# Moving the output gate's projection and the keys' rotation in the first mixer of a two-block transformer

## Chip, cores and metric

One core of a Trainium2 chip runs the whole program. The metric is device time in microseconds, the median of three executions. TensorE is PE in the rows, VectorE DVE, ScalarE ACT, GpSimd POOL, SyncE SP.

## What is computed

The reference is a model of two blocks in float32 on 256 tokens (`x`) with 256 context tokens; later come two more attention layers with experts. The change lies in the first block's mixer alone. There `h` (256 tokens) and `hx` (256 context tokens), both 1024 wide, are multiplied by one matrix of 3600 columns, which gives the queries, keys and values of a neighbourhood attention, those of an mLSTM, an output gate and the mLSTM's input and forget gates:

```python
qa, ka, va, qb, kb, vb, ob, g = jnp.split(h @ w_in, SPLITS, axis=-1)
y_a = neighbourhood_attention(qa, ka, va, kax, vax, rpb)
h_b, _ = mlstm_bidirectional(axial_rope(qb), axial_rope(kb) * k_scale, vb, li, lf, ...)
y = jnp.concatenate([y_a, rms_norm(h_b, head_g) * sigmoid(ob)], -1) @ w_out
```

The mLSTM runs over four chunks of 128 tokens (two of them context) in two directions and with four heads. Per chunk it updates a state by `outer(k * a_tok, v)`, where `a_tok` comes from running sums and maxima of the gates, and then reads it. The output gate `ob` is needed for the 256 tokens of `x` only, and only at the end.

## The kernel before

Everything in float32 goes as two parts (`hh` high, `hl` low; a weight tile as `wh` and `wl`), so each product is three matmuls. The weights stream from memory in the order in which TensorE uses them, in slabs of 16 tiles of 128x128. A slab lands in `raw`, ScalarE copies its high part to `wh` (L1414, `split_upto`) and VectorE subtracts to get `wl` (L2080). There are three buffers of `wh` and `wl`, so slab i is split once slab i-3 has been used. Each engine runs a program written out by hand in one order, and waits on counters of what the others have done. `taken(n)` in the programs of ScalarE and VectorE stands where n tiles begin to be used, and splits the slabs that come three later: where it stands is where those engines do that work.

`mixer0` exists once per engine (TensorE L738, ScalarE L1575, VectorE L2390). On TensorE the order is:

1. query columns `naq` of the attention (`x` only), then its values `nav` (`project_tok`, all 512 tokens), keys `nak` with the attention worked in between, and the gates `mgate`;
2. the mLSTM's queries `mq` (into `mqT`) and keys `mk` (into `mkT`), the rotation of the queries (`rotate("rotq")`: two matmuls with the permutation `swap`, then four VectorE operations), and the values' projection `mv` (to `mva`);
3. `cc`: 20 small transposes of the gates' rows, and `ap`: four small matmuls. They wait for "rows", the end of the running sums and maxima of the gates on VectorE (L2470 to L2480, eight rounds) and of their exponentials on ScalarE;
4. the rotation of the keys (`rotk`), the output gate's projection `og` (two blocks of 128 tokens, 48 matmuls, two slabs), the turning of the rotated keys (`kt`, 16 transposes, L803) and of the attention's results (`turn_out`, 8 transposes, L700);
5. the 16 `outer` products, each of which waits for a scaled key `mKS` of ScalarE (L1650), then the loop over the reads of the state, with the output projection `mout` in between.

Of PSUM there are 8 banks, given out in turn: who takes a bank waits until its last content has been read.

Of the kernel before, what the change touches and what calls it, by code (L numbers as in the profile page):

```python
# [13 lines left out]
P = 128  # L14
D = 1024
KC = 8
# [103 lines left out]
def program(nc, dram):  # L120
# [88 lines left out]
    with ExitStack() as mx:  # L209
# [13 lines left out]
        with ExitStack() as ph:  # L223
# [3 lines left out]
            ml.og = sb(ph, "mog", [P, 2, 512])  # L227
            ml.cs = const(ph, "mlcs", [P, 2, T])
            ml.swap = const(ph, "swap", [P, P])
# [19 lines left out]
            ml.ss = sb(ph, "mss", [P, 3, 8])  # L249
        ml.CR, ml.AR, ml.WR, ml.ER = ml.IR, ml.FR, ml.t1, ml.BR  # L250
# [147 lines left out]
    fold_at = {2: HALF, 3: 0, 4: HALF, 5: HALF, 6: 0}  # L398
# [9 lines left out]
    def tensor_program(e):  # L408
# [303 lines left out]
        def project_tok(name, c0, ncol, blocks, h, by, *key, steps=0):  # L712
# [7 lines left out]

        def h_part(k):
            return hh[:, k, 0:T], hl[:, k, 0:T]

# [14 lines left out]
        def mixer0():  # L738
# [8 lines left out]
            st.kept.remove(bank_of["roots", 1])  # L747
            project_tok("min", 8, 512, 4, h, act_out, "nav")
# [32 lines left out]
            project_tok("min", 20, 512, 4, h, act_out, "mv")  # L781
# [14 lines left out]
            rotate("rotk", ml.kT)  # L796
            project_tok("min", 24, 512, 2, h, act_out, "og")
            result.mark("h read", "mix0")
            for hd in range(4):
                b = bank(("kt", hd), act_out, "kt", hd)  # L800
                w.wait_ge(dve_out, "rotk", "done")
                for ch in range(4):
                    ins = e.transpose(b[:, P * ch:P * ch + P], ml.kT[:, hd, P * ch:P * ch + P], ident[:])  # L803
                ins.then_inc(*result("kt", hd))
# [19 lines left out]
            def weights(i):  # L824
# [5 lines left out]
                sel, k = hh[:, hd, HALF:HALF + P], 4 + 2 * d + ch  # L830
                mm(b[:, 0:2 * P], sel, hh[:, k, 0:2 * P], True, False)
                mm(b[:, 0:2 * P], sel, hl[:, k, 0:2 * P], False, True)
# [20 lines left out]
            def part(d, ks):  # L853
                b = banks[bank_of["mout", d]][:, T * (d % 2):T * (d % 2) + T]
                for k in ks:
                    w.wait_ge(dve_out, "turn l", "mix0", k)
                    wmm(("mout", d, k), b, *h_part(k), k == 0 and d % 2 == 0, k == KC - 1, "mout", d)
# [542 lines left out]
    def scalar_program(e):  # L1400
# [169 lines left out]
        def turn_out(name, c, h_free):  # L1570
            w.wait_ge(result, "turn", name, c)
            w.wait_ge(result, "h read", *h_free)
            e.activation(hh[:, c, 0:T], banks[bank_of["turn", name, c]][:, 0:T], ACT.Copy).then_inc(*act_out("turn h", name, c))

        def mixer0():  # L1575
            taken(4 * KC)
            taken(4 * KC)
# [40 lines left out]
            taken(4 * KC)  # L1618
            w.wait_ge(result, "mv")
# [3 lines left out]
            taken(4 * KC)  # L1623
            w.wait_ge(result, "og")
            for q in range(2):
                act(ml.og[:, q, :], banks[bank_of["og", q]][:], ACT.Sigmoid, key=("og", q))
            for h in range(4):
                w.wait_ge(result, "kt", h)
                act(X[:, h // 2::2, T + P * (h % 2):T + P * (h % 2) + P],
                    banks[bank_of["kt", h]][:].rearrange("p (c k) -> p c k", k=P), ACT.Copy, key=("kt", h))  # L1630

            for c in range(4):
                turn_out("mix0", c, ["mix0"])
            w.wait_ge(const_in["sel4"], 0)
            w.wait_ge(act_out, "rows")
            e.activation(hh[:, 0:4, HALF:HALF + P], ml.sel[:], ACT.Copy).then_inc(*act_out("sel"))
# [1894 lines left out]
```

## Time and profile before

| | us |
|---|---|
| median of three runs | 2453.25 |
| the three runs | 2447.88, 2453.25, 2453.5 |
| profiled execution, its own time | 2445.76 |
| span of its trace | 2444.0 |
| PE busy in it | 2316.0 (95%) |
| DVE busy | 1696.2 (69%) |
| ACT busy | 1197.4 (49%) |
| first mixer, first to last projection | 481 to 740 |

The profiled execution has 1.76 us more than its span. The page gives averages over all stages; since TensorE is busy nearly throughout, what matters for a change in one stage is which gaps TensorE has there, and what ended them. In rows of the trace "[4.72 <-ACT mKS L1650]" says that the engine was idle for 4.72 us and that ScalarE's write of `mKS` ended it; x16 counts instructions that were merged into the row.

### The profile page before, as it was taken

The numbers are of one execution on the slowest core, as the hardware profiler recorded it, in microseconds if no ns is written. First come the engines' busy times: TensorE is split into PE (matmuls) and PEld (weight loads), VectorE is DVE, ScalarE is ACT, GpSimd is POOL, SyncE is SP. The second block draws the span as 40 slices with busy tenths as digits, with TensorE's granted clock in tenths as the row PEclk, the third lists the DMA queues.
The fourth block names the chain that finished last, engine by engine and source line by source line (L and its number), as shares of the span: only waits on it lengthen the run. The fifth ranks groups of instructions, "written<-read, shape, count | busy, mean of one in ns | idle before, by whom it ended". The sixth has DMA issues, their size and how long they took to land.

```text
span 2444.0 us, 33909 instructions
## 1 busy us (share of the span) xinstructions
PE 2316.0 (95%) x14128; PEld 2026.8 (83%) x14128; DVE 1696.2 (69%) x2260; ACT 1197.4 (49%) x1549; POOL 168.0 (7%) x270
## 2 busy tenths in 40 slices
PE   7999999899989999999999998979999889899997
PEld 3778888778779999999999997968888778688886
DVE  5897676743676666666666655568888776688886
ACT  3221212344544454445544454547666666576665
POOL 0111111021000000000000002200000002000000
PEclk9999999999999999999999999989999989999999
DMA  7777887432214454456434454229888732389884
GB/s 277 226 239 254 268 271 257 156 129 99 86 53 156 174 206 170 174 192 227 178 139 173 173 204 141 104 85 354 330 317 322 298 104 71 129 336 348 311 315 167
DMA packets 80534, 501.71 MB, mean 205 GB/s; under 512 B 9584, under 2 KB 10688, under 8 KB 28656
## 3 DMA queue, kind: packets, MB, share of 16 engines
q1 hardware_dynamic: 59120, 423.66, 47.0%
q0 software_dynamic: 21248, 75.75, 9.9%
q8 instruction: 115, 1.88, 0.3%
q14 instruction: 51, 0.42, 0.0%
HBM read 498.33 MB, written 1.05 MB: 204 GB/s over the span
## 4 chain that ended last, share of the span: by engine, by line
PE 65%; DVE 19%; ACT 10%; issue 4%; DMA 1%; DVEq 0%; SPq 0%; ACTq 0%
PE bank L416 63%; DVE wl L2080 8%; ACT wh L1414 6%; DVE macc L2116 1%; ACT s L1515 1%; DVE f L2297 1%; DMA mring<-in_wmod 1%; DVE s L2288 1%; PE bank L653 1%; DMA raw<-in_wmod 1%; DVE rs L2140 1%; PE bank L1286 1%; DVE hl L2272 0%; ACT H L1524 0%; DVE tmpm L2265 0%
## 5 line engine op out<-in xcount | busy, mean ns | idle before, releaser
L2080 DVE TENSOR_TENSOR wl<-raw,wh 128x2048 fp32r<-128x2048 f32 (+1 forms) x437 | 904.9, 2076 | 379.9 <-ACT wh L1414 375.8
L1414 ACT ACTIVATE wh<-raw 128x2048 fp32r<-128x2048 f32 (+1 forms) x437 | 756.4, 1738 | 302.9 <-PE bank L416 302.5
L416 PE MATMUL bank<-hh,wh 128*128 128x258 f32 (+2 forms) x2200 | 688.8, 313 | 32.7 <-ACT o_rl L1843 5.3
L416 PE MATMUL bank<-hh,wl 128*128 128x258 f32 (+2 forms) x2200 | 672.9, 306 | 0.0
L416 PE MATMUL bank<-hl,wh 128*128 128x258 f32 (+2 forms) x2200 | 671.2, 305 | 0.0
L416 PEld LDWEIGHTS bank<-hh,wh 128*128 128x128 f32 x2200 | 419.2, 191 | 63.2 <-issue 7.3
L416 PEld LDWEIGHTS bank<-hl,wh 128*128 128x128 f32 x2200 | 419.7, 191 | 18.2 <-issue 0.5
L416 PEld LDWEIGHTS bank<-hh,wl 128*128 128x128 f32 x2200 | 418.4, 190 | 18.8
L416 PE MATMUL bank<-wh,hh 128*128 128x512 f32 (+1 forms) x704 | 277.6, 394 | 7.6 <-DVE wl L2080 4.7
L416 PE MATMUL bank<-wh,hl 128*128 128x512 f32 (+1 forms) x704 | 274.6, 390 | 0.0
L416 PE MATMUL bank<-wl,hh 128*128 128x512 f32 (+1 forms) x704 | 274.3, 390 | 0.0
L416 PE MATMUL bank<-H,wh 128*128 128x256 f32 (+1 forms) x704 | 219.1, 311 | 2.2 <-DVE L L2307 2.0
L416 PE MATMUL bank<-H,wl 128*128 128x256 f32 (+1 forms) x704 | 217.7, 309 | 0.0
L416 PE MATMUL bank<-L,wh 128*128 128x256 f32 (+1 forms) x704 | 217.7, 309 | 0.0
L2116 DVE SCALAR_TENSOR_TENSOR macc<-mring,c_cvec,macc 128x1024 f32<-128x1024 f32 x140 | 175.7, 1282 | 44.8 <-DMA mring<-in_wmod 39.8
L416 PEld LDWEIGHTS bank<-wh,hh 128*128 128x128 f32 x704 | 133.3, 189 | 40.1 <-issue 5.5
L416 PEld LDWEIGHTS bank<-wl,hh 128*128 128x128 f32 x704 | 133.1, 189 | 29.6
L416 PEld LDWEIGHTS bank<-wh,hl 128*128 128x128 f32 x704 | 133.2, 189 | 27.8 <-issue 0.2
L416 PEld LDWEIGHTS bank<-H,wh 128*128 128x128 f32 x704 | 132.6, 188 | 12.2 <-DVE L L2307 3.1
L416 PEld LDWEIGHTS bank<-H,wl 128*128 128x128 f32 x704 | 132.6, 188 | 8.1
L416 PEld LDWEIGHTS bank<-L,wh 128*128 128x128 f32 x704 | 132.6, 188 | 7.8
L1524 ACT ACTIVATE H<-f 128x256 fp32r<-128x256 f32 (+1 forms) x88 | 41.5, 471 | 192.5 <-DVE f L2304 150.8
(472 smaller groups left out, 2651.1 us busy)
## 6 DMA issues: line engine op xcount, KB each, us to landing
raw<-in_wstream SPq DMA_DIRECT2D x393, 1024.0 KB, 4.9
mring<-in_wmod POOLq DMA_DIRECT2D x128, 512.0 KB, 4.5
raw<-in_wmod SPq DMA_DIRECT2D x6, 1024.0 KB, 6.8
X<-in_xT SPq DMA_DIRECT2D x1, 2048.0 KB, 12.5
mods<-in_wmod SPq DMA_DIRECT2D x2, 1024.0 KB, 19.0
bias<-in_nabias POOLq DMA_DIRECT2D x16, 128.0 KB, 2.5
c_sglg<-in_sglg POOLq DMA_DIRECT2D x1, 1024.0 KB, 4.9
c_sglb<-in_sglb POOLq DMA_DIRECT2D x1, 1024.0 KB, 6.9
```

The source lines that it names most:

```text
L416: return e.matmul(out, lhsT, rhs, start=start, stop=stop, skip_group_check=True)
L653: ins = e.transpose(b[:, P * k:P * k + P], a.E[:, v % 4, P * k:P * k + P], ident[:])
L1286: ins = e.transpose(banks[b][:, P * c:P * c + P], q.H[:, s_, P * c:P * c + P], ident[:])
L1414: e.activation(wh[i % NB][:, o], raw[i % NR][:, o], ACT.Copy).then_inc(*slab_high(st.split + m))
L1515: e.activation(s_, s_, ACT.Silu, bias=f.s[:, i % 2, T:T + 1]).then_inc(*act_out("silu", u, i))
L1524: e.activation(f.H[:, i - f0, :], f.f[:, i % 2, 0:n], ACT.Copy).then_inc(*act_out("H", u, i))
L2080: e.tensor_tensor(wl[i % NB][:, o], raw[i % NR][:, o], wh[i % NB][:, o].bitcast(F32), ALU.subtract).then_inc(*slab_low(st.split + m))
L2116: e.scalar_tensor_tensor(acc, src, c, acc, ALU.mult, ALU.add).then_inc(*dve_out("block", n, who))
L2140: e.reciprocal(rs[:, o:o + T], rs[:, o:o + T]).then_inc(*dve_out("rs", nm, i))
L2288: e.tensor_tensor(f.s[:, i % 2, :], banks[bank_of["fin", u, i, 0]][:, 0:W1], rs[:, 0:W1], ALU.mult).then_inc(*dve_out("rooted a", u, i))
L2297: e.scalar_tensor_tensor(f.f[:, i % 2, 0:T], f.f[:, i % 2, 0:T], f.f[:, i % 2, T:T + 1], f.s[:, i % 2, 0:T], ALU.add, ALU.mult).then_inc(* ...
```

## The change

The projection `og` moves from behind the values' projection to right behind `naq`, and its sigmoid with it on ScalarE. The rotation of the keys moves to TensorE's second step (of eight) of the values' projection, and on VectorE to right behind the rotation of the queries. The turning of the keys moves into the seventh step. On ScalarE the copies of the turned keys come ahead of the values' copies, and the rows' parts ahead of the turned results. Buffers are laid out anew: `og` gets room beside the attention's buffers, the selection rows get a tile of their own (`mrow`), and the turned results use other columns of `hh` and `hl`.

```diff
 # TensorE, mixer0
             st.kept.remove(bank_of["roots", 1])
+            project_tok("min", 24, 512, 2, lambda k: h_of(1, 1, k), act_out, "og")
             project_tok("min", 8, 512, 4, h, act_out, "nav")
...
             rotate("rotq", ml.qT)
-            project_tok("min", 20, 512, 4, h, act_out, "mv")
+            def beside_values(k):
+                if k == 0:
+                    st.kept.update(bank_of["mv", q] for q in range(4))
+                if k == 1:
+                    rotate("rotk", ml.kT)
+                if k == 6:
+                    turn_keys()
+
+            project_tok("min", 20, 512, 4, h, act_out, "mv", middle=beside_values)
...
-            rotate("rotk", ml.kT)
-            project_tok("min", 24, 512, 2, h, act_out, "og")
-            result.mark("h read", "mix0")
-            for hd in range(4):
-                b = bank(("kt", hd), act_out, "kt", hd)
-                w.wait_ge(dve_out, "rotk", "done")
...
 # ScalarE, mixer0
             taken(4 * KC)
+            taken(4 * KC)
+            w.wait_ge(result, "og")
+            for q in range(2):
+                act(ml.og[:, q, :], banks[bank_of["og", q]][:], ACT.Sigmoid, key=("og", q))
...
             act_out.mark("rows")
             taken(4 * KC)
+            w.wait_ge(const_in["sel4"], 0)
+            w.wait_ge(dve_out, "rotk", "done")
+            e.activation(ml.row[:], ml.sel[:], ACT.Copy).then_inc(*act_out("sel"))
+            for h in range(4):
+                w.wait_ge(result, "kt", h)
+                act(X[:, h // 2::2, T + P * (h % 2):T + P * (h % 2) + P],
+                    banks[bank_of["kt", h]][:].rearrange("p (c k) -> p c k", k=P), ACT.Copy, key=("kt", h))
             w.wait_ge(result, "mv")
...
-            taken(4 * KC)
-            w.wait_ge(result, "og")
...
 # VectorE, mixer0
             rotate("rotq", ml.qT)
+            rotate("rotk", ml.kT)
             w.wait_ge(act_out, "softplus", 2)
...
-            rotate("rotk", ml.kT)
-            taken(4 * KC)
```

**VectorE behind the keys' evacuation.** `sq`, `mqT` and `mkT` are the rotations, `mFR` and `mBR` begin the gates' sums. Before:

```order
L2432 TENSOR_SCALAR mkT<-bank 128x512 x4
L2439 TENSOR_TENSOR sq<-bank,c_mlcs 128x512 x2
L2442 TENSOR_TENSOR mqT<-mqT,c_mlcs 128x1024
L2444 TENSOR_TENSOR mqT<-mqT,sq 128x1024
L2449 TENSOR_SCALAR mFR<-mFR 4x1024
L2451 TENSOR_TENSOR mFR<-mFR,mt 4x1024
```

With the change:

```order
L2445 TENSOR_SCALAR mkT<-bank 128x512 x4
L2452 TENSOR_TENSOR sq<-bank,c_mlcs 128x512 x2
L2455 TENSOR_TENSOR mqT<-mqT,c_mlcs 128x1024
L2457 TENSOR_TENSOR mqT<-mqT,sq 128x1024
L2452 TENSOR_TENSOR sq<-bank,c_mlcs 128x512 x2
L2455 TENSOR_TENSOR mkT<-mkT,c_mlcs 128x4x256
L2457 TENSOR_TENSOR mkT<-mkT,sq 128x4x256
L2463 TENSOR_SCALAR mFR<-mFR 4x1024
```

The four operations on `mkT` stood behind the copies to `mCC` and now stand ahead of all work on the gates.

**ScalarE from the last exponential of the gates (`mt`) to the scaled keys (`mKS`).** `wh` are splits of slabs, `X` the turned keys, `mva` the values, `hh<-bank` the turned results. Before:

```order
L1434 ACTIVATE mt<-mMR,mmr 4x128
L1414 ACTIVATE wh<-raw 128x2048 x2
L1621 ACTIVATE mva<-bank 128x4x128 x4
L1414 ACTIVATE wh<-raw 128x2048 x2
L1434 ACT_TABLE_LOAD
L1434 ACTIVATE mog<-bank 128x512 x2
L1434 ACTIVATE X<-bank 128x4x128 x4
L1573 ACTIVATE hh<-bank 128x256 x4
L1636 ACTIVATE hh<-c_sel 128x4x128
L1638 ACTIVATE hh<-mMR 4x4x128
L1638 ACTIVATE hh<-mt 4x4x128
L1650 ACTIVATE mKS<-X,mCC 128x128 x16
```

With the change:

```order
L1446 ACTIVATE mt<-mMR,mmr 4x128
L1426 ACTIVATE wh<-raw 128x2048 x2
L1637 ACTIVATE mrow<-c_sel 128x512
L1446 ACTIVATE X<-bank 128x4x128 x4
L1644 ACTIVATE mva<-bank 128x4x128 x4
L1648 ACTIVATE hh<-mMR 4x4x128
L1648 ACTIVATE hh<-mt 4x4x128
L1585 ACTIVATE hh<-bank 128x256 x4
L1662 ACTIVATE mKS<-X,mCC 128x128 x16
L1670 ACTIVATE mW<-mW 128x128
```

Two splits, a table load and the gate's sigmoids are gone from between, and all the rest is still ahead of the first `mKS`.

**TensorE at the end of the values' projection, with the numbers of the PSUM banks.** With the change (two rows of the seventh step, the turned keys, three of the eighth step, then `cc`, `ap` and the results):

```order
L418 MATMUL bank4<-wh2,hl 128x512
L418 MATMUL bank4<-wl2,hh 128x512
L788 MATMUL bank7<-c_ident,mkT 128x128 x4
L788 MATMUL bank0<-c_ident,mkT 128x128 x4
L788 MATMUL bank5<-c_ident,mkT 128x128 x4
L788 MATMUL bank6<-c_ident,mkT 128x128 x4
L418 MATMUL bank1<-wh2,hh 128x512
...
L418 MATMUL bank4<-wl2,hh 128x512
L809 MATMUL bank7<-c_ident,mIR 128x4
...
L418 MATMUL bank0<-map,c_sel4 128x8 x4
L702 MATMUL bank1<-c_ident,Y 128x128 x2
```

The transposes of `cc` now take bank 7, in which the first head's turned keys lie until ScalarE has copied them to `X`; before they took bank 5, long free, and 48 matmuls of `og` stood behind them. The results `Y` are turned behind `ap`, as before, not inside the values' projection.

## Rows read from the trace of the kernel before

**Rows 1.** The page: span and number of instructions.
```profile
span 2444.0 us, 33909 instructions
```

**Rows 2.** Windows: stretch, us, busy us (count) of PE PEld DVE ACT POOL, clock, DMA.
```profile
496.70:522.00 25.30, 25.30 (x97) 20.32 (x98) 9.90 (x11) 3.03 (x2) 5.53 (x6) 0.88 0.54 187
...
644.60:667.30 22.70, 17.98 (x106) 14.65 (x105) 15.81 (x21) 16.30 (x24) 0.00 (x0) 0.99 0.51 185
```

**Rows 3.** Waits of PE, 480 to 740: us in total, times, longest.
```profile
PE bank L416 <- ACT mKS L1650: 4.7, 1, 4.7
PE bank L416 <- DVE wl L2080: 3.8, 1, 3.8
```

**Rows 4.** Timeline of PE: start, us, engine, line, operation, names, shape, count, idle before.
```profile
620.53 1.96 PE L416 MATMUL bank<-mqT,c_swap 128*128 128x512 f32 x4 [0.83 <-DVE mkT L2432]
...
622.55 0.40 PE L416 MATMUL bank<-wh,hl 128*128 128x512 f32 x1
...
644.62 0.22 PE L789 MATMUL bank<-c_ident,mIR 4*128 4x4 f32 x1
...
646.84 1.98 PE L416 MATMUL bank<-mkT,c_swap 128*128 128x512 f32 x4
...
659.76 1.91 PE L803 MATMUL bank<-c_ident,mkT 128*128 128x128 f32 x16
...
667.26 1.20 PE L416 MATMUL bank<-mva,mKS 128*128 128x129 f32 x4 [4.72 <-ACT mKS L1650]
```

**Rows 5.** Timeline of DVE: the queries' rotation, and the end of the gates' rows.
```profile
621.76 1.45 DVE L2439 TENSOR_TENSOR sq<-bank,c_mlcs 128x512 f32<-128x512 f32 x2 [1.33 <-PE bank L416]
...
624.50 1.22 DVE L2444 TENSOR_TENSOR mqT<-mqT,sq 128x1024 f32<-128x1024 f32 x1
625.83 0.68 DVE L2449 TENSOR_SCALAR mFR<-mFR 4x1024 f32<-4x1024 f32 x1
...
642.07 0.28 DVE L2480 TENSOR_TENSOR mBR<-mBR,mMR 4x128 f32<-4x128 f32 x1
645.41 4.49 DVE L2080 TENSOR_TENSOR wl<-raw,wh 128x2048 fp32r<-128x2048 f32 x2 [3.06 <-ACT wh L1414]
```

**Rows 6.** Timeline of ACT from the end of the gates' rows to the first scaled keys.
```profile
643.48 3.69 ACT L1414 ACTIVATE wh<-raw 128x2048 fp32r<-128x2048 f32 x2
647.20 2.07 ACT L1621 ACTIVATE mva<-bank 128x512 f32<-128x512 f32 x4
649.13 1.94 ACT L1414 ACTIVATE wh<-raw 128x2048 fp32r<-128x2048 f32 x1
...
661.28 1.98 ACT L1434 ACTIVATE X<-bank 128x512 f32<-128x512 f32 x3
...
664.12 1.21 ACT L1573 ACTIVATE hh<-bank 128x256 fp32r<-128x256 f32 x4
665.17 0.66 ACT L1636 ACTIVATE hh<-c_sel 128x512 fp32r<-128x512 f32 x1
665.69 0.61 ACT L1638 ACTIVATE hh<-mMR 4x512 fp32r<-4x512 f32 x1
...
666.73 0.97 ACT L1650 ACTIVATE mKS<-X,mCC 128x128 f32<-128x128 f32 x3
```

**Rows 7.** Timeline of DVE behind the attention's queries: splits of three slabs.
```profile
494.24 4.49 DVE L2080 TENSOR_TENSOR wl<-raw,wh 128x2048 fp32r<-128x2048 f32 x2 [1.32 <-ACT wh L1414]
...
502.50 2.29 DVE L2080 TENSOR_TENSOR wl<-raw,wh 128x2048 fp32r<-128x2048 f32 x1
```

**Rows 8.** Timeline of ACT: table load ahead of the first weights.
```profile
673.83 1.28 ACT L1658 ACT_TABLE_LOAD   x1
675.31 0.31 ACT L1658 ACTIVATE mW<-mW 128x128 f32<-128x128 f32 x1 [0.20 <-DVE mW L2533]
```

**Rows 9.** Windows over the outer products and behind them.
```profile
666.60:673.40 6.80, 6.14 (x27) 6.17 (x28) 5.21 (x14) 5.91 (x16) 0.00 (x0) 0.50 0.00 0
673.40:680.00 6.60, 6.17 (x50) 5.84 (x50) 4.50 (x15) 4.62 (x11) 0.00 (x0) 1.00 0.01 2
```

More of the change, by code:

```diff
@@ L249, in program @@
             ml.ss = sb(ph, "mss", [P, 3, 8])
+            ml.og = sb(ph, "mog", [P, 2, 512])
+            with ExitStack() as pre:
+                ml.cs = const(pre, "mlcs", [P, 2, T])
+                ml.swap = const(pre, "swap", [P, P])
+            ml.row = sb(ph, "mrow", [P, 4, P], F32R)
         ml.CR, ml.AR, ml.WR, ml.ER = ml.IR, ml.FR, ml.t1, ml.BR
@@ L710, in project, with project_tok @@
                         attend(1)
-        def project_tok(name, c0, ncol, blocks, h, by, *key, steps=0):
+        def project_tok(name, c0, ncol, blocks, h, by, *key, steps=0, middle=None):
             bs = [bank((*key, q), by, *key, q) for q in range(blocks)]
@@ L780, in mixer0, with turn_keys @@
             rotate("rotq", ml.qT)
-            project_tok("min", 20, 512, 4, h, act_out, "mv")
+            def turn_keys():
+                for hd in range(4):
+                    b = bank(("kt", hd), act_out, "kt", hd)
+                    w.wait_ge(dve_out, "rotk", "done")
+                    for ch in range(4):
+                        ins = e.transpose(b[:, P * ch:P * ch + P], ml.kT[:, hd, P * ch:P * ch + P], ident[:])
+                    ins.then_inc(*result("kt", hd))
+            def beside_values(k):
[6 more added lines that the diff above has]
+            project_tok("min", 20, 512, 4, h, act_out, "mv", middle=beside_values)
+            st.kept.difference_update(bank_of["mv", q] for q in range(4))
+            result.mark("h read", "mix0")
             b = bank(("cc",), dve_out, "cc")
@@ L1622, in mixer0 @@
                              ACT.Copy).then_inc(*act_out("mv", q))
-            taken(4 * KC)
-            w.wait_ge(result, "og")
[L1625 to L1630, printed above, removed]
-            for c in range(4):
[L1633 to L1636, printed above, removed]
-            for kind, R in enumerate((ml.MR, ml.WR)):
-                e.activation(hh[0:4, 4:8, P * kind:P * kind + P].rearrange("p (d c) t -> p d c t", d=2),
-                             R[:, :, 0:T].rearrange("p d (c t) -> p d c t", c=2), ACT.Copy).then_inc(*act_out("row parts", kind))
+            w.wait_ge(act_out, "rows")
+            for kind, R in enumerate((ml.MR, ml.WR)):
+                e.activation(hh[0:4, 4:8, T + P * kind:T + P * kind + P].rearrange("p (d c) t -> p d c t", d=2),
+                             R[:, :, 0:T].rearrange("p d (c t) -> p d c t", c=2), ACT.Copy).then_inc(*act_out("row parts", kind))
+            for c in range(4):
+                turn_out("mix0", c)
             def scaled_keys(n, unit):
@@ L2495, in mixer0 @@
                           banks[bank_of["ap",]][:, 0:32].rearrange("p (h d s) -> p h d s", d=2, s=4)).then_inc(*dve_out("ap"))
-            rotate("rotk", ml.kT)
-            taken(4 * KC)
+            for kind, R in enumerate((ml.MR, ml.WR)):
+                w.wait_ge(act_out, "row parts", kind)
+                c = slice(T + P * kind, T + P * kind + P)
+                e.tensor_tensor(hl[0:4, 4:8, c].rearrange("p (d c) t -> p d c t", d=2),
+                                R[:, :, 0:T].rearrange("p d (c t) -> p d c t", c=2),
+                                hh[0:4, 4:8, c].rearrange("p (d c) t -> p d c t", d=2).bitcast(F32),
+                                ALU.subtract).then_inc(*dve_out("row parts", kind))
+            for c in range(4):
+                turn_out("mix0", c)
             def update(n, unit):
```

41 lines of the change are left out of this document (15 added, 26 removed).

## Prediction

> **What bounds the kernel now.** The span is 2444.0 us [rows 1], and TensorE is busy for nearly all of it, so I went to the one stage that the change touches and asked where TensorE stands still there. The list of its waits from 480 to 740 us [rows 3] has two that the change can reach. 3.8 us go to a split of a slab (`wl`) right behind the attention's query columns, where `og` now comes in. 4.7 us go to the first scaled key `mKS`, in front of the outer products. The windows [rows 2] show the same: from 644.6 to 667.3 TensorE is busy for 17.98 of 22.70 us, and elsewhere around the moved parts it is full. All else in the stage is TensorE's own work, and the change removes none of it: it is the same matmuls in another order. So the question is only what becomes of the waits.
>
> For the 4.7 us the timelines are read side by side. TensorE rotates the queries at 620.53, runs the 96 matmuls of the values, begins `cc` at 644.62, rotates the keys at 646.84, turns them from 659.76, and starts the outer products at 667.26 [rows 4]. VectorE ends the queries' rotation at 625.72, works on the gates from 625.83, and its last operation there starts at 642.07 [rows 5]. ScalarE ends the gates' exponentials and goes on to the slabs at 643.48, and scales the first key at 666.73 [rows 6]. So the gates' rows are ready 1.1 us before TensorE asks for them at 644.62: that chain, rotation, gates, exponentials, is as long as the values' projection, and `og` behind it gives ScalarE 11 us in which to do everything else.
>
> **The change, part by part.**
>
> *Size of `og`.* From the second matmul of the values at 622.55 to `cc` at 644.62 there are 95 steps, 0.232 us each [rows 4]. 48 such are 11.1 us. As a check: rotation of the keys and `og` take 659.76 - 646.84 = 12.92 us, a rotation takes 622.55 - 620.53 - 0.23 = 1.8 us, and 11.1 are left.
>
> *`og` in its new place: 11.1 us later for all behind it, and no more.* It starts where the values `nav` started, at the same slab, so the wait of 3.8 us stays as it is. The stretch of lower clock behind that wait (0.88 over 496.7 to 522.0 [rows 2]) lasts, I take it, as long with `og` under it. `og` uses a slab in half the time of `nav`: 24 matmuls. The first is used up no sooner than 5.6 us after 496.7 at full clock (24 x 0.232), the second is split at 494.24 + 4.49 = 498.7, the third at 502.50 + 2.29 = 504.8 [rows 7], and it is wanted no sooner than 496.7 + 11.1 = 507.8. So the splits keep ahead by 3 us or more. What if not: one split of 2.29 us is lost. Nothing is gained either, bound 0. The gate's sigmoids, 1.3 us and a table load of 1.28 us on ScalarE, lie beside `nav`.
>
> *VectorE: the gates' rows come 7.4 us later.* The keys' rotation now stands ahead of the gates on VectorE, and it cannot begin until TensorE's `swap` matmuls, which stand behind two of eight steps of the values. The 25th matmul would start at 622.55 + 23 x 0.232 = 627.9. From the start of the `swap` matmuls to the end of the rotation it is 625.72 - 620.53 = 5.2 us [rows 4, 5]. That ends at 633.1, and the gates' first operation starts at 633.2 instead of 625.83: 7.4 us later, of which about 3.3 are VectorE standing still and the rest its work. The gates' chain itself is unchanged, so VectorE's and ScalarE's ends of it move by the same 7.4 us.
>
> *ScalarE: from the end of the gates to the first scaled key.* Before, 666.73 - 643.48 = 23.25 us, mostly waiting for `og` and its sigmoids. Now everything stands in one row behind the gates, in ScalarE's order: two slabs 3.72 (643.48 to 647.20), the selection rows 0.52, the turned keys 4 x 0.66 (1.98 for 3), the values 1.93 (647.20 to 649.13), the rows' parts 1.04 for two, the turned results 1.05 (664.12 to 665.17) [rows 6]. That is 10.9 us.
>
> *TensorE behind the values.* It ends them, with rotation and turning inside (1.8 and 1.9 us), at 644.62 + 3.7 + 11.1 = 659.4. `cc` waits for the gates and also, since it takes the bank of the first turned keys, for ScalarE's copy of them: 643.48 + 7.4 + 11.1 = 662.0 for the slabs, then 3.72 + 0.52 + 0.66, so 666.9. TensorE stands still for about 7.5 us there, then again between the turned results. The results are turned into the banks of the values as ScalarE empties them; the last of these is empty 2.1 us before ScalarE asks for the results, so this hides. `cc` and `ap` take 2.2 us at full clock (644.62 to 646.84); at half clock up to 4.5, which makes the turned results late by 0.5 us at most. Bound: 0 and 0.5; I take 0, as 20 transposes of 4 columns each have little in them that a clock could slow. VectorE's copies of `cc` lie beside ScalarE's values.
>
> *Sum.* The first scaled key, and with it the outer products and all behind, moves by 7.4 (gates) + 10.9 (new row on ScalarE) - 23.25 (old) + 11.1 (`og` ahead of it) = **+6.2 us**. Against the profiled execution's own 2445.76 this is 2452.0. That execution is below all three runs shown, and 7.5 us below their median; on the median 2453.25 it gives **2459.5**, 0.25% more. About 0.3%, or 7.4 us, is what a measurement can tell from no change, so the likeliest finding is "the same", on the slow side.
>
> *The table load.* ScalarE's load at 673.83 goes away, since the sigmoid no longer stands between the exponentials. It ends at 675.11, and the row behind it starts at 675.31 and was released by VectorE's `mW`, not by the load [rows 8]. I take 0; the other bound is 1.28 us. The Trainium skill ("ScalarE: Activation LUTs", "What ACT_TABLE_LOAD costs") gives 2.66 us for each switch of a set, load and drain together; by it the sum would be +3.5. The row speaks against that here: it fits between two instructions that wait for others.
>
> *Clock.* The outer products run at 0.50 of the clock before, 1.2 GHz [rows 9]; TensorE stood still for 4.72 us ahead of them. With 7.5 us of standing still and then a few small matmuls I expect the same again. There 27 matmuls took 6.14 us, two to a product, so 0.45 us a product and 7.3 for 16. If the clock were back for them, this would go down at most to ScalarE's pace of 0.33 (0.97 for 3 [rows 6]), 5.3 us: 2.0 less. If it stayed low longer, the stage behind, 6.60 us at full clock [rows 9], would lose a part: its waits for other engines hide some, so up to 2.
>
> **The rivals.**
>
> - *The clock is back before the outer products.* +6.2 - 2.0 = +4.2 us. For it: `cc`, `ap` and the results keep TensorE active ahead of them. Against: before, it was still at 0.50 up to 673.4, though TensorE had worked densely from 667.26 on [rows 4, 9].
> - *The page's rule on table loads holds.* +3.5 us, from above; against it the row of the load.
> - *More is lost.* A late slab in the early part (2.3) or a low clock for longer (up to 2): about +8.3 us. For it: the longer gap; against: 3 us of room in the splits.
> - *Faster: TensorE is the bound behind the values.* If the gates' rows are done before the values' projection ends, the wait for `mKS` shrinks: ScalarE has only values, rows' parts, results and the key ahead (1.93 + 1.04 + 1.05 + 0.53 = 4.6 us) from TensorE's end at 659.4, so outer products at 664.0 instead of 667.26: -3.3 us. That needs ScalarE done with gates, slabs and turned keys by 659.4. The rows put this at 668.9 (662.0 + 3.72 + 0.52 + 2.64), 9.5 us too late. It decides from the point where VectorE's gates would start 9.5 us sooner, which no row shows.
> - *The change doesn't do what it says:* the results are turned behind `ap`, not inside the values' projection, as the order shows. This is in the sum.
>
> **How the numbers follow.** Forecast 0.60, clock back 0.12, table rule 0.03, more lost 0.18, faster 0.07. The forecast's own spread is 1 us, and a median of three moves by some 2.5 us: the runs of before alone span 5.6 us. From the forecast's +6.2 to the bound of 7.4 it is 1.2 us, so some 0.35 of its chance falls above; of "more lost" some 0.75. That gives slower 0.36. Faster by over 7.4 us comes only from the faster case with a lucky median: 0.02. The rest is 0.62. The range goes from the faster clock with the low runs, 2452, to "more lost" with the high ones, 2465.5; the faster case and the two tails are left out.
>
> **What would show it.** Right: on VectorE the keys' rotation at about 639 to 644 us with idle time ahead of it, and the gates' first operation about 18.5 us later than before (644.3); TensorE's wait at `cc` of 7 to 8 us, released by ScalarE's `X`; the wait for `mKS` smaller than 4.7; the outer products at about 673.4; the early wait of 3.8 us unchanged, no gap inside `og` or `nav`; stages behind 740 us shifted and not changed. Wrong: `cc` following the values without a gap (then the gates' chain is not what bounds), a new wait for `wl` from 497 to 534, or a change of over 2 us behind the mixer.

## The result, and the profile after

| | before | after |
|---|---|---|
| median of 16 runs of each, us | 2450.77 | 2457.03 |
| the runs, us | 2443.49 to 2455.99 | 2450.7 to 2459.47 |
| ratio, 95% interval | | 1.0026 [1.0019, 1.0034] |
| span of the profiled execution, us | 2444.0 | 2454.0 |

The changed kernel is 6.3 us slower by the medians. The two profiled spans are 10.0 us apart, and the trace says how much of that is the change's. The attention's first query column starts at 482.78 us instead of 481.29, and nothing ahead of it was changed. From there to the last product with the gate on VectorE (`Y<-Y,mog`, the end of what the change touches) it takes 240.34 us instead of 235.67. From that product to the end of the span it is 1730.9 instead of 1727.0. So 4.7 us lie in the stage of the change, and 5.3 outside it. How much of either is chance is shown under the experiments.

The page of the changed kernel, its first lines:

```profile
span 2454.0 us, 33910 instructions
...
PE 2322.7 (95%) x14128; PEld 2033.8 (83%) x14128; DVE 1697.2 (69%) x2260; ACT 1195.7 (49%) x1548; POOL 167.9 (7%) x270
```

The waits of PE from 480 to 750 us, the counterpart of [rows 3]. Lines have moved: L418 is the old L416, L2092 the old L2080, L1662 the old L1650, L809 the first small transpose of `cc`.

```profile
PE bank L809 <- ACT X L1446: 7.5, 1, 7.5
...
PE bank L418 <- DVE wl L2092: 3.7, 1, 3.7
...
PE bank L418 <- ACT mKS L1662: 0.8, 1, 0.8
```

The reader is to see that the wait for the first scaled key has almost gone, 4.7 to 0.8 us, and that a larger one has taken its place 6.7 us ahead of the first outer product. The wait of 3.7 for `wl` is nearly as before. It ends where the gate's projection now starts, and behind it the list of PE's waits is empty up to 536 us, so neither this projection nor the one behind it met a late slab.

Timeline of PE, the queries' rotation to the outer products, the counterpart of [rows 4]:

```profile
631.69 1.96 PE L418 MATMUL bank<-mqT,c_swap 128*128 128x512 f32 x4 [0.83 <-DVE mkT L2445]
...
638.98 1.88 PE L418 MATMUL bank<-mkT,c_swap 128*128 128x512 f32 x4
...
654.60 1.91 PE L788 MATMUL bank<-c_ident,mkT 128*128 128x128 f32 x16
...
666.82 0.26 PE L809 MATMUL bank<-c_ident,mIR 4*128 4x4 f32 x1 [7.52 <-ACT X L1446]
...
670.75 1.97 PE L702 MATMUL bank<-c_ident,Y 128*128 128x128 f32 x8
...
673.48 6.95 PE L418 MATMUL bank<-mva,mKS 128*128 128x129 f32 x32 [0.76 <-ACT mKS L1662]
```

VectorE and ScalarE beside it, the counterparts of [rows 5] and [rows 6]. VectorE's timeline, with the keys' rotation now ahead of the gates:

```profile
635.67 1.22 DVE L2457 TENSOR_TENSOR mqT<-mqT,sq 128x1024 f32<-128x1024 f32 x1
640.10 1.48 DVE L2452 TENSOR_TENSOR sq<-bank,c_mlcs 128x512 f32<-128x512 f32 x2 [3.21 <-PE bank L418]
...
642.88 1.22 DVE L2457 TENSOR_TENSOR mkT<-mkT,sq 128x1024 f32<-128x1024 f32 x1
644.21 0.68 DVE L2463 TENSOR_SCALAR mFR<-mFR 4x1024 f32<-4x1024 f32 x1
```

ScalarE's timeline, the row of work from the end of the gates' exponentials to the first scaled keys:

```profile
661.86 3.69 ACT L1426 ACTIVATE wh<-raw 128x2048 fp32r<-128x2048 f32 x2
665.46 0.61 ACT L1637 ACTIVATE mrow<-c_sel 128x512 fp32r<-128x512 f32 x1
666.16 2.66 ACT L1446 ACTIVATE X<-bank 128x512 f32<-128x512 f32 x4
668.72 2.06 ACT L1644 ACTIVATE mva<-bank 128x512 f32<-128x512 f32 x4
670.63 0.61 ACT L1648 ACTIVATE hh<-mMR 4x512 fp32r<-4x512 f32 x1
671.15 0.61 ACT L1648 ACTIVATE hh<-mt 4x512 fp32r<-4x512 f32 x1
671.67 1.47 ACT L1585 ACTIVATE hh<-bank 128x256 fp32r<-128x256 f32 x4
673.04 0.97 ACT L1662 ACTIVATE mKS<-X,mCC 128x128 f32<-128x128 f32 x3
```

No row here shows idle time of ScalarE ahead of it: ScalarE is the chain. TensorE's 7.52 us are the time in which it has nothing to do and ScalarE works off what stands behind the gates.

Windows (stretch, us, busy us and count of PE, PEld, DVE, ACT, POOL, clock, DMA), first over the early part, the counterpart of [rows 2], then over this stretch, the counterpart of [rows 9]:

```profile
496.90:522.00 25.10, 23.91 (x97) 19.42 (x98) 14.46 (x13) 8.61 (x7) 6.77 (x8) 0.93 0.66 236
...
661.80:666.70 4.90, 0.00 (x0) 0.00 (x0) 2.91 (x2) 4.81 (x5) 0.00 (x0) 0.50 0.00 0
666.80:670.70 3.90, 3.88 (x28) 3.89 (x28) 2.13 (x7) 3.66 (x8) 0.00 (x0) 0.50 0.83 309
...
673.40:680.00 6.60, 6.52 (x31) 6.34 (x31) 5.08 (x16) 5.64 (x16) 0.00 (x0) 0.59 0.00 0
680.00:690.00 10.00, 9.45 (x75) 8.80 (x74) 6.81 (x24) 4.80 (x16) 0.00 (x0) 1.00 0.01 2
```

Inside the long wait the granted clock falls to 0.50, 1.2 GHz. It is so under `cc` and `ap` too, and for most of the outer products. Before, only the outer products had it.

### The profile page after: what moved, and what is told of

It is laid out like the page before. It is cut to its first block, busy times and chain, and to the rows that moved or that the text cites. A ratio compares the mean times of both kernels' runs of the same rounds, so it can differ in the third digit from the quotient of the medians.

```text
span 2454.0 us, 33910 instructions
## 1 busy us (share of the span) xinstructions
PE 2322.7 (95%) x14128; PEld 2033.8 (83%) x14128; DVE 1697.2 (69%) x2260; ACT 1195.7 (49%) x1548; POOL 167.9 (7%) x270
## 3 DMA queue, kind: packets, MB, share of 16 engines
HBM read 498.33 MB, written 1.05 MB: 203 GB/s over the span
## 4 chain that ended last, share of the span: by engine, by line
PE 64%; DVE 20%; ACT 10%; issue 4%; DMA 1%; DVEq 0%; SPq 0%; ACTq 0%
PE bank L418 63%; DVE wl L2092 8%; ACT wh L1426 6%; DVE macc L2128 1%; ACT s L1527 1%; DVE f L2309 1%; DMA mring<-in_wmod 1%; DVE s L2300 1%; PE bank L655 1%; DMA raw<-in_wmod 1%; PE bank L1298 1%; DVE rs L2152 1%; DVE hl L2284 0%; ACT H L1536 0%; DVE tmpm L2277 0%
## 5 line engine op out<-in xcount | busy, mean ns | idle before, releaser
L2092 DVE TENSOR_TENSOR wl<-raw,wh 128x2048 fp32r<-128x2048 f32 (+1 forms) x437 | 906.0, 2079 | 384.1 <-ACT wh L1426 380.4
L418 PE MATMUL bank<-hh,wh 128*128 128x258 f32 (+2 forms) x2200 | 689.6, 313 | 30.9 <-ACT o_rl L1855 5.3
L418 PE MATMUL bank<-hh,wl 128*128 128x258 f32 (+2 forms) x2200 | 674.6, 307 | 0.0
L418 PE MATMUL bank<-hl,wh 128*128 128x258 f32 (+2 forms) x2200 | 673.1, 306 | 0.0
L418 PEld LDWEIGHTS bank<-hh,wh 128*128 128x128 f32 x2200 | 420.9, 191 | 61.2 <-DVE hl L2712 6.0
L418 PEld LDWEIGHTS bank<-hl,wh 128*128 128x128 f32 x2200 | 421.0, 191 | 18.1 <-issue 0.5
L418 PEld LDWEIGHTS bank<-hh,wl 128*128 128x128 f32 x2200 | 420.0, 191 | 18.7
L418 PE MATMUL bank<-wh,hh 128*128 128x512 f32 (+1 forms) x704 | 277.5, 394 | 7.5 <-DVE wl L2092 4.6
L418 PE MATMUL bank<-wh,hl 128*128 128x512 f32 (+1 forms) x704 | 274.1, 389 | 0.0
L418 PE MATMUL bank<-wl,hh 128*128 128x512 f32 (+1 forms) x704 | 274.1, 389 | 0.0
L418 PE MATMUL bank<-H,wh 128*128 128x256 f32 (+1 forms) x704 | 219.3, 311 | 2.4 <-DVE L L2319 2.1
L418 PE MATMUL bank<-H,wl 128*128 128x256 f32 (+1 forms) x704 | 217.9, 310 | 0.0
L418 PE MATMUL bank<-L,wh 128*128 128x256 f32 (+1 forms) x704 | 217.9, 310 | 0.0
L418 PEld LDWEIGHTS bank<-wh,hh 128*128 128x128 f32 x704 | 133.2, 189 | 39.5 <-DVE wl L2092 4.3
L418 PEld LDWEIGHTS bank<-wl,hh 128*128 128x128 f32 x704 | 132.9, 189 | 29.3
L418 PEld LDWEIGHTS bank<-wh,hl 128*128 128x128 f32 x704 | 133.1, 189 | 27.6 <-issue 0.5
L418 PEld LDWEIGHTS bank<-H,wh 128*128 128x128 f32 x704 | 132.7, 188 | 12.3 <-DVE L L2319 3.2
L418 PEld LDWEIGHTS bank<-H,wl 128*128 128x128 f32 x704 | 132.7, 188 | 8.0
L418 PEld LDWEIGHTS bank<-L,wh 128*128 128x128 f32 x704 | 132.7, 189 | 7.8
```

The lines of the kernel that those rows point to most:

```text
L418: return e.matmul(out, lhsT, rhs, start=start, stop=stop, skip_group_check=True)
L2092: e.tensor_tensor(wl[i % NB][:, o], raw[i % NR][:, o], wh[i % NB][:, o].bitcast(F32), ALU.subtract).then_inc(*slab_low(st.split + m))
```

## The experiments

Each kernel was timed beside the kernel before, 7 to 12 executions of each new one. Since the code ahead of the stage and behind it is the same in all of them, I read each trace by starts relative to the queries' first `swap` matmul. In the table "early" is the time from the attention's first query column to that matmul, "gates" the start of VectorE's first gate operation behind it, then the start of `cc`, of the first outer product, and of VectorE's last product with the gate. "Stage" is early plus that last one, less before's 235.67. The last column is the measured ratio less one, times before's 2451.

| | early | gates | `cc` | outer | last gate product | stage, us more | measured, us more |
|---|---|---|---|---|---|---|---|
| before | 139.24 | 5.31 | 24.09 | 46.73 | 96.43 | | |
| after | 148.90 | 12.52 | 35.13 | 41.79 | 91.44 | +4.7 | +6.4 |
| e1 | 148.99 | 9.15 | 34.31 | 40.97 | 90.30 | +3.6 | +4.7 |
| e2 | 150.20 | 18.08 | 40.67 | 47.33 | 96.80 | +11.3 | +9.6 |
| e3 | 150.06 | 12.53 | 31.52 | 41.47 | 90.65 | +5.0 | +6.1 |
| e4 | 150.07 | 5.31 | 24.09 | 41.72 | 90.82 | +5.2 | +5.1 |
| e5 | 148.72 | 9.15 | 31.76 | 38.51 | 88.00 | +1.1 | -0.2 |
| e6 | 148.81 | 9.15 | 29.96 | 36.71 | 85.92 | -0.9 | -1.2 |
| e7 | 138.02 | 5.31 | 24.09 | 41.86 | 92.43 | -5.2 | -2.7 |
| e8 | 137.83 | 12.52 | 35.12 | 55.68 | 103.86 | +6.0 | +5.6 |
| e9 | 139.01 | 5.31 | 24.09 | 41.89 | 92.48 | -4.2 | -4.2 |
| e10 | 139.20 | 5.31 | 24.09 | 41.86 | 93.40 | -3.1 | -5.1 |

The stage tells the measured time to within 2.5 us in every row. Outside the stage the code is the same but for its shift, and there the twelve traces give 480.5 to 486.1 us ahead of it and 1726.9 to 1736.4 behind it. The 1.5 and 3.8 us that the changed kernel has more there are within this spread; nothing shows them to be the change's.

The column "early" has a chance part too. Over the 25 us behind the wait of 3.7 us the granted clock is 0.93 or 0.94 in after, e1 and e5 to e8, and 0.88 or 0.89 in before, e2 to e4, e9 and e10, and both groups have kernels with the gate's projection there and without it. Like compared with like, the projection costs 11.0 to 11.1 us (148.90 against 137.83, 150.07 against 139.01), and the lower clock some 1.2, in before 1.3. Had before's trace had the higher one, the stages of the first group would be 1.3 us more: +6.0 for after, +4.9 for e1, +2.4, +0.4, -3.9 and +7.3 for e5 to e8.

**e1 and e2: where the keys' rotation stands.** The theory was that VectorE's gates' rows hang on it, and the end of the stage on them. e1 takes TensorE's `rotate("rotk")` from the second step of the values to ahead of them, e2 puts it at the fourth step.

```diff
 # e1
             rotate("rotq", ml.qT)
+            rotate("rotk", ml.kT)
...
-                if k == 1:
-                    rotate("rotk", ml.kT)
 # e2
-                if k == 1:
+                if k == 3:
                     rotate("rotk", ml.kT)
```

> The changed kernel with one line moved: TensorE's two swap matmuls for the keys stand right behind those for the queries, ahead of the values' projection, instead of behind its second step. Theory (the first outer product is set by a chain: VectorE's rotation of the keys, the gates' rows behind it, then ScalarE's row of 10.9 us of copies and splits): VectorE no longer stands still for 3.2 us between the two rotations, the gates' first operation starts 3.5 us sooner, TensorE's wait at the gates' transposes falls from 7.5 to about 4, and the time from the queries' swap matmuls to the first outer product falls from 41.8 to about 38.3 us: 3.4 us less than the changed kernel, about 2.8 us more than before (ratio 1.001). Rival (og in its new place, or the clock, is what costs): no difference to the changed kernel, 41.8 us and ratio 1.0026.

> The opposite dose: the changed kernel with the keys' swap matmuls two steps of the values' projection later, behind the fourth of eight. Theory (chain through the keys' rotation): two steps are 24 matmuls of 0.232 us, so all behind comes 5.6 us later: VectorE stands still for about 8.8 us between the rotations, the first outer product is 47.3 us behind the queries' swap matmuls instead of 41.8, total about 11.8 us over before (ratio 1.0048). Rival (og in its new place, or the clock): as the changed kernel, ratio 1.0026.

e2: ratio 1.0039 [1.0025, 1.0053], with the expected 1.0048 inside. Two steps of 12 matmuls are 24 x 0.232 = 5.6 us; the gates start 5.56 later (18.08 against 12.52), `cc` and the outer products 5.54. The wait in e2:

```profile
672.57 0.26 PE L809 MATMUL bank<-c_ident,mIR 4*128 4x4 f32 x1 [13.07 <-ACT X L1446]
```

e1: ratio 1.0019 [1.0009, 1.0028]. The gates do start 3.4 us sooner, and the outer products only 0.8, at 40.97 where 38.3 was expected. Timelines of PE and of ACT in e1:

```profile
666.20 0.26 PE L808 MATMUL bank<-c_ident,mIR 4*128 4x4 f32 x1 [6.70 <-ACT mva L1643]
```

```profile
663.00 2.66 ACT L1445 ACTIVATE X<-bank 128x512 f32<-128x512 f32 x4
665.56 2.06 ACT L1643 ACTIVATE mva<-bank 128x512 f32<-128x512 f32 x4
667.47 0.61 ACT L1647 ACTIVATE hh<-mMR 4x512 fp32r<-4x512 f32 x1
667.98 0.61 ACT L1647 ACTIVATE hh<-mt 4x512 fp32r<-4x512 f32 x1
670.86 1.66 ACT L1584 ACTIVATE hh<-bank 128x256 fp32r<-128x256 f32 x4 [2.26 <-PE bank L702]
```

I had missed what else the edit moves. Banks are given out in turn, so with the rotation's two banks taken ahead of the values' four, `cc` falls on a bank that the values hold. It is released by ScalarE's copy `mva` instead of its first `X`, 2.6 us later in ScalarE's row, and then the turned results are late for ScalarE by 2.26 us.

**e3: the key copies ahead of ScalarE's two slabs.** The rival theory was that `cc` is late only through its bank, and that releasing this sooner would bring the outer products forward.

```diff
 # ScalarE
             act_out.mark("rows")
-            taken(4 * KC)
...
                     banks[bank_of["kt", h]][:].rearrange("p (c k) -> p c k", k=P), ACT.Copy, key=("kt", h))
+            taken(4 * KC)
```

> The changed kernel with ScalarE's order changed behind the gates: selection rows and the four copies of the turned keys first, the two splits of slabs behind them. It frees the bank for which TensorE waits 7.5 us sooner and takes nothing off ScalarE's row. Theory (ScalarE's whole row of 10.9 us between the gates and the first scaled key is what counts): TensorE's wait at the gates' transposes falls to about 3.8 us, a wait for the scaled keys of 4 to 4.5 us takes its place, the first outer product stays at 41.8 us (within 0.5) behind the queries' swap matmuls, ratio as the changed kernel, 1.0026. Rival (the bank of the turned keys is the cause, since the largest wait in the trace is there): 3.7 us less than the changed kernel, ratio 1.001.

Ratio 1.0025 [1.0013, 1.0037]. `cc` starts 3.6 us sooner, and the outer products at 41.47 instead of 41.79. The waits of PE in e3 show nearly the same time, 7.6 us for 8.3, in three pieces:

```profile
PE bank L809 <- ACT X L1446: 3.9, 1, 3.9
...
PE bank L702 <- ACT mva L1644: 2.1, 1, 2.1
PE bank L418 <- ACT mKS L1662: 1.6, 1, 1.6
```

So the bank names the place of the wait, and the length of ScalarE's row sets when it all ends.

**e4 and e8: one half of the change each.** e4 is the kernel before with the gate's projection and sigmoid moved as in the change, and nothing else of it. e8 is the changed kernel with the gate's projection put back behind `ap`, its sigmoid and splits with it.

```diff
 # e4, from the kernel before
+            project_tok("min", 24, 512, 2, lambda k: h_of(1, 1, k), act_out, "og")
             project_tok("min", 8, 512, 4, h, act_out, "nav")
...
-            project_tok("min", 24, 512, 2, h, act_out, "og")
 # e8, from the changed kernel
-            project_tok("min", 24, 512, 2, lambda k: h_of(1, 1, k), act_out, "og")
...
             ins.then_inc(*result("ap"))
+            project_tok("min", 24, 512, 2, h, act_out, "og")
```

> The kernel before with og's projection and sigmoid alone moved behind the query columns; rotation and turning of the keys stay where they were, behind the gates' transposes. Theory (og was the cover under which ScalarE and VectorE did splits, copies and the keys' rotation): TensorE waits about 6 us for the rotation of the keys on VectorE before it can turn them, and about 3 us more for the scaled keys; the first outer product comes about 40.5 us behind the queries' swap matmuls, where the kernel before has 46.7 less 11.1 of og, 35.6: 4.9 us more than before, ratio 1.002. Rival (moving og is harmless and the rotation's move ahead of the gates is the whole cost): ratio 1.000 or below.

> The other half of the change by itself: keys are rotated and turned beside the values' projection as in the changed kernel, and the gate's projection stands behind ap as before the change. Times in us behind the queries' first swap matmul. Theory (the key rotation delays the gates' rows by 7 us; cc waits 7.5 us for ScalarE on TensorE whatever the gate's projection does, and its 11 us come behind that): cc starts near 35.1, ap ends near 39, the gate's projection ends near 50, the first outer product starts at 51 to 54 against 46.7 before: ratio to before 1.002 to 1.003. Rival (this half is good or harmless and the whole loss is that of the gate's move, as the run with the gate's move alone, 1.0021, could be read): first outer product at 47 or sooner, ratio 1.0000 or less.

e4: 1.0021 [1.0012, 1.0029]; e8: 1.0023 [1.0014, 1.0032]. Neither half is good or harmless by itself, and both together (1.0026) cost hardly more than one. Waits of PE, first in e4, then in e8:

```profile
PE bank L803 <- DVE mkT L2445: 6.0, 1, 6.0
...
PE bank L416 <- ACT mKS L1650: 2.7, 1, 2.7
```

```profile
PE bank L807 <- ACT X L1446: 7.5, 1, 7.5
...
PE bank L418 <- DVE hl L2388: 1.9, 1, 1.9
```

In e4 the outer products came at 41.72, where 40.5 was expected. The projection no longer covers VectorE's rotation of the keys nor ScalarE's row, 8.7 us of standing still. Behind the wait of 6.0 the clock is 0.50 from 665 to 668 us, and the turning of the keys takes 3.44 us up to the next row (665.16 to 668.60) instead of 1.74 (659.76 to 661.50): more than the missing 1.2. In e8 `cc` waits as long as in the changed kernel, and the gate's projection stands behind this wait and covers too little. It also takes 13.7 us there (660.22 to 673.90) instead of 11.1, since the clock is 0.50 from 656 to 664 us and 0.80 from 664 to 668. e8's outer products came at 55.68, above the 51 to 54 expected; the ratio was as expected.

**e5 and e6: the changed kernel mended.** e5 is e1 with the row of banks moved on by four, so that `cc` takes a bank of the turned keys. e6 also makes half of ScalarE's slab copies ahead of the gates' loop.

```diff
 # e5: e1 and
             st.kept.difference_update(bank_of["mv", q] for q in range(4))
+            st.turn += 4
 # e6: e5 and
             act(ml.t1[:], ml.t1[:], ACT.Ln, bias=1.0, key=("softplus", 2))
             taken(2 * KC)
+            taken(2 * KC)
...
             act_out.mark("rows")
-            taken(4 * KC)
+            taken(2 * KC)
```

> The keys' swap matmuls stand right behind the queries', and the row of banks is moved on by four behind the values, so that the cumulative sums (cc) take bank 7, which holds turned keys, and the next product (ap) bank 0, and none takes a bank of the values. All times in us behind the queries' first swap matmul. Theory (the run before failed by its bank only): VectorE's gates start at 9.2 as there, ScalarE's gates' rows end at 26.9, cc is released by ScalarE's first key copy at about 31.8 instead of 34.3, the first scaled key ends near 37.8 and the first outer product starts near 38.3, against 41.8 in the changed kernel: 3 us less than the changed kernel, ratio to before about 1.0012 (1.0003 to 1.0020). Rival (the gates' rows on VectorE are not what the chain hangs on; ScalarE's weight splits and copies in their order are): the first outer product stays at 41 or later, ratio 1.002 or more.

> As the run before it, and of ScalarE's sixteen weight roundings (four slabs' worth) that stood between the gates' rows and the key copies, half are made ahead of the gates' loop, in ScalarE's idle time behind the softplus. Times in us behind the queries' first swap matmul. Theory: ScalarE reaches the key copies 1.9 us (half of the 3.7 of two slabs) sooner, cc is released near 29.9, the first outer product starts near 36.4; ratio to before about 1.0004 (0.9996 to 1.0012). Rival: the roundings ahead of the gates push the gates' own start on ScalarE by the same 1.9 us, and the outer product stays at 38.3, the ratio at that of the run before it.

e5: 0.9999 [0.9988, 1.001]; e6: 0.9995 [0.9987, 1.0004]. The outer products came within about 0.3 us of the theory (38.51 for 38.3, 36.71 for 36.4). The ratios are lower than it had: for e5 1.0003 to 1.0020 was expected, for e6 0.9996 to 1.0012. PE's wait at `cc` in e5, then in e6:

```profile
662.19 0.26 PE L809 MATMUL bank<-c_ident,mIR 4*128 4x4 f32 x1 [4.16 <-ACT X L1446]
```

```profile
659.28 0.26 PE L809 MATMUL bank<-c_ident,mIR 4*128 4x4 f32 x1 [2.35 <-ACT X L1446]
```

From 7.52 through 4.16 to 2.35 us, every microsecond taken out of the chain ahead of ScalarE's copy `X` comes out of the wait. The loss of the change is thus shown to hang on the chain that ends in this copy: two steps more put 5.5 us on it (e2), 3.4 and 5.2 us less bring the outer products forward by 3.3 and 5.1. Mended, the kernel ties with before within the intervals; by the stages at like clock e5 still has 2.4 us more and e6 0.4.

The waits alone are not the whole sum. From the queries' `swap` to the first outer product TensorE has, without the 11.1 us of the gate's projection, 30.9 us of work and 4.7 of waiting before, and 33.5 and 8.3 after. Of the 6.2 us that these are apart 3.6 are waiting, and 2.6 are TensorE's own work at the lower clock: `cc` and `ap` take 3.93 us (666.82 to 670.75) instead of 2.22, the turned results 1.97 instead of 1.04. In e1, e2, e5 and e6 the work is 33.5 as well, with 7.5, 13.8, 5.0 and 3.2 us of waiting. In all of them TensorE still waits 0.8 to 0.9 us for the first scaled key, so ScalarE's row ends last, and faster work would mostly have been more waiting.

**e7, e9 and e10: another order.** Before, the gate's projection hides the rotation of the keys and ScalarE's row up to the key copies, but the turning and all that follows stand uncovered behind it. e7 leaves the projection there and turns the keys inside it, at its fifth step, and the results at its seventh; ScalarE's first three scaled keys come ahead of the sigmoids. e9 is e7 with e6's half of the slab copies early. e10 is e7 with the sigmoids behind all 16 scaled keys, and the gate's banks held till then.

```diff
 # e7, TensorE, behind ap
+            def beside_gate(k):
...
+                if k == 4:
+                    turn_keys()
                 if k == 6:
-                    turn_keys()
+                    w.wait_ge(dve_out, "y", "na", 1)
+                    for c in range(4):
+                        turn_out("mix0", Y, c)
...
+            rotate("rotk", ml.kT)
+            project_tok("min", 24, 512, 2, h, act_out, "og", middle=beside_gate)
```

> Another order, meant to beat both: the output gate's projection stays where it was before the change (behind ap and the keys' rotation), and the keys are turned at its fifth step, the attention's results at its seventh; ScalarE copies the keys and scales the first three ahead of the gate's sigmoids. Times in us behind the queries' first swap matmul. Theory (the change costs because the 11 us of the gate's projection no longer cover ScalarE's and VectorE's row; and the old order lost 4.7 us because nothing covered the last of ScalarE's row): the wait of 4.7 us for the first scaled key goes, the first outer product starts near 42.3 against 46.7 before; ratio to before 0.998 (0.9970 to 0.9990). Rival (TensorE's granted clock is at its lower level for much of this stretch whatever the order, so the gate's projection takes some 3 to 5 us more where it stands): first outer product at 45 to 47, ratio 0.9995 to 1.0005. Rival 2 (ScalarE's sigmoids, now between scaled keys, hold up the fourth): the wait comes back inside the outer products, 3 us or more in one gap.

> The kernel of the run before (gate's projection late, keys and results turned inside it), with half of ScalarE's slab roundings made ahead of the gates' loop as in the run with the split. Times in us behind the queries' first swap matmul. Theory (ScalarE's row is what the fourth outer product waits 1.85 for): the row gets 1.9 shorter where it counts, the wait falls below 0.5, the weights' first exponent argument on VectorE starts at 48.5 to 49 instead of 50.4; ratio to before 0.998 to 0.9985. Rival (ScalarE waits there for TensorE's projection and key turn, 2.4 us in its row, and the table load and sigmoids stand behind these): nothing moves, the wait stays at 1.5 or more and the ratio at 0.999.

> The gate late as in the same kernel, and its two sigmoids (with the table load ahead of them, 2.5 us together) moved behind all sixteen scaled keys; the gate's two banks are held until the outer products are out. Times in us behind the queries' first swap matmul. Theory (the wait of 1.85 in the outer products is the table load and the sigmoids): the wait goes, VectorE's first weight argument starts near 48.5 instead of 50.4, ratio to before 0.998 to 0.9985. Rival (six banks instead of eight for the outer products, or the load moved onto the path of the first exponent): the sixteen outer products take as long or the first weight's exponent is late by the 2.5 us, and the ratio stays at 0.999 or above.

e7: 0.9989 [0.9979, 0.9999]; e9: 0.9983 [0.9972, 0.9993]; e10: 0.9979 [0.997, 0.9988]. All three are faster than before, by 3 to 5 us, and by 9 to 12 than the change (their intervals overlap, so I name no best one). The outer products start at 41.86, where 42.3 was expected. That is 4.9 us sooner than before; VectorE's first weight argument, behind them, comes at 50.38, 4.0 sooner. The difference is the second rival, whose gap is 1.85 us where 3 or more was put. PE and ACT in e7:

```profile
666.00 0.83 PE L418 MATMUL bank<-mva,mKS 128*128 128x129 f32 x6
668.68 5.33 PE L418 MATMUL bank<-mva,mKS 128*128 128x129 f32 x26 [1.85 <-ACT mKS L1657]
```

```profile
663.58 0.99 ACT L1657 ACTIVATE mKS<-X,mCC 128x128 f32<-128x128 f32 x3
664.48 1.18 ACT L1585 ACTIVATE hh<-bank 128x256 fp32r<-128x256 f32 x4
665.73 1.28 ACT L1446 ACT_TABLE_LOAD   x1
667.03 1.23 ACT L1446 ACTIVATE mog<-bank 128x512 f32<-128x512 f32 x2
668.15 5.26 ACT L1657 ACTIVATE mKS<-X,mCC 128x128 f32<-128x128 f32 x13
```

The fourth outer product waits for table load and sigmoids. e9 and e10 were to remove this, and neither did: in e9 ScalarE waits for TensorE's turned keys all the same, 4.2 us instead of 2.4, and the wait of 1.8 stays; in e10 it moves to the sigmoid's bank, which the first read of the state now needs:

```profile
669.75 0.54 PE L418 MATMUL bank<-hh,mrow 128*128 128x256 f32 x1 [2.03 <-ACT mog L1446]
```

VectorE's first weight argument comes at 50.43 in e9 and 50.71 in e10, where about 48.5 was expected in both. So in e9 the rival's mechanism held. In e10 the theory was right on the outer products, and the gain was lost behind them: to the held banks, which the rival had named in another place. Both ratios are nevertheless those of the theories, 0.998 to 0.9985. The traces don't explain this: at like clock e9's stage is e7's, and e10's is 1 us longer.

## Why the prediction was right, step by step

The forecast was +6.2 us; measured are +6.3 by the medians, and the ratio's interval is +4.7 to +8.3. The time itself was forecast as 2459.5, on a median of three, 2453.25; the median of 16 executions of before is 2450.77, and the changed kernel's 2457.03 lies as much below the forecast. By its steps:

- *`og` is 11.1 us in its new place.* In e2, e3 and e4 the early part is 10.8 to 11.0 longer than before, as forecast. In the changed kernel's own trace it is 9.66, and 9.5 to 9.8 in e1, e5 and e6. The difference goes with the clock: there the stretch from 496.9 to 522 has 0.93 of the clock where before had 0.88 [rows 2]. e8, without the projection there, has the higher clock too and shows the same 1.4 less than before (137.83). So this is luck of the trace, and it accounts for most of the difference between the 4.7 in the trace and the forecast's 6.2.
- *VectorE's gates 7.4 later, about 3.3 of it idle:* 12.52 - 5.31 = 7.2, and 3.21 idle. Right.
- *ScalarE's row of 10.9:* from 661.86 to 673.04 it is 11.2. The turned results took 1.37 from their start to the next row's instead of 1.05; TensorE turned them in 1.97 us at the lower clock. This is the bound of 0 to 0.5 of which I had taken 0, for the reason that small transposes have little that a clock could slow. That reason was wrong: the 20 of `cc` took 0.11 us each instead of 0.063, and `cc` and `ap` 3.93 us, near the bound of 4.5.
- *`cc` released by `X` after about 7.5:* 7.52, and outer products at 673.48, where 673.4 was forecast. The second agreement is closer than it deserves: a start 1.5 later than before's and an early part 1.4 shorter cancel in it. Relative to the queries' rotation the first outer product moved by 41.79 - 46.73 = -4.9, and forecast was 6.2 - 11.1 = -4.9.
- *Same clock for the outer products:* 16 took 6.95 us, where 7.3 was forecast and 5.3 would have been the rival's; at full clock e10 shows 5.60 for them (row in the last section). So the rival "the clock is back" did not happen, and its 2.0 us would have been 1.4.
- *Table load, 0:* from outer product to last gate product nothing was gained, 91.44 - 41.79 = 49.65 against 96.43 - 46.73 = 49.70. ScalarE stood still ahead of the first `mW` for 1.65 us, waiting for VectorE, where the load had been. The Trainium skill ("ScalarE: Activation LUTs", "What ACT_TABLE_LOAD costs") gives about 2.66 us for a switch, load and drain together, which would have made it +3.5 in all; the measured +6.4 [+4.7, +8.3] leaves that out. Its 1.28 us for the load agree with the rows. Its total does not: in e7 the copies in front of the load end at 665.66 and the sigmoids behind it start at 667.03, so the switch took 1.37 us, and the measurement decides. e7 also has a load that costs something: there it stands between scaled keys, and TensorE waits 1.85.
- *The early part meets no late slab:* the wait is 3.7 us for 3.8, and there is none behind it up to 536.

What the prediction had wrong is less in its sum than in how it speaks of the parts. It adds 11.1, 7.4 and 10.9 and takes off 23.25, which is right for the two moves together; it does not see that each move alone costs about 5 us (e4, e8). Both uncover the same row of ScalarE, and who reads the terms one by one would expect 11 and 7. Nor does it ask where the new order breaks even. With one microsecond won for each taken off the chain, its own numbers put this at 6.2 us, and its rival "faster", 3.3 us below before, at 9.5. e5 and e6, with 3.4 and 5.2 us taken off, fit this line by their stages at like clock (+2.4 and +0.4, where it gives +2.8 and +1.0), and by the measured ratios they are already level with before.

## What to carry to other kernels

Work that has no dependence on its neighbours is a cover: before moving it, add up what the other engines do behind it and ask what will cover that. Here 11 us of matmuls were taken away from beside ScalarE's row and put where TensorE had no wait left to cover (busy for all of the 25.30 us [rows 2]); putting the dependent small steps inside the cover (e7) gained, and taking the cover away lost. Where banks go round in turn, an edit on one place changes who waits for whom further on, so the order of banks has to be written down again for each variant, as e1 showed.

## What was not expected of the hardware

The stretch at 1.2 GHz was longer than before, and it began sooner; the forecast had only asked whether it would end later. Before, TensorE's clock was at 0.50 under most of the outer products, from 666.6 to 673.4 us, and full behind them [rows 9]. After, it was at 0.50 from 661.8 us, inside the wait, to 678.8, through `cc`, `ap`, the turned results and most of the outer products: 17 us instead of 6.8. Its price was small here, since ScalarE's row was longer anyway; in e4 and e8 it accounts for outer products later than expected. In e10, where TensorE has no gap from the values to the outer products, the clock is full under them. The row of the 16 outer products in e10, and windows over the end of the gate's projection, the outer products, and the wait behind them:

```profile
662.11 5.60 PE L418 MATMUL bank<-mva,mKS 128*128 128x129 f32 x32
...
655.00:662.00 7.00, 7.00 (x45) 6.08 (x44) 6.01 (x8) 6.09 (x13) 0.00 (x0) 1.00 0.57 227
662.10:667.70 5.60, 5.46 (x33) 4.46 (x31) 4.90 (x16) 4.91 (x14) 0.00 (x0) 1.00 0.21 86
667.70:671.00 3.30, 1.27 (x7) 1.28 (x7) 0.38 (x2) 3.19 (x4) 0.00 (x0) 0.81 0.00 0
```

In e10 the order without a gap thus gave back the clock as well as the wait: 5.60 us for all 16 instead of 6.95. In e8, with the projection between the long wait and the outer products, these took 5.62.
